# Weight-block sums in the second half of a feed-forward: from GpSimd to VectorE, spread over the steps

## The chip, the cores and the metric

The kernel runs on one core of a Trainium2 chip. The metric is the time of one launch on the device in microseconds (us), given as the median of several runs. Five engines matter here: TensorE (PE, with its weight loads as PEld), VectorE (DVE), ScalarE (ACT), GpSimd (POOL) and the queue SP, which issues all DMAs. Each works through its own instruction list in order and waits on semaphores.

## The reference

The reference is one layer of a hybrid encoder on 1024 tokens of width 1024. What matters here is its feed-forward, with DFF = 2816:

```
hn = rms_norm(h)
ab = hn @ w_in                       # 1024 x 1024 @ 1024 x 5632
a, g = ab[:, :2816], ab[:, 2816:]
u = gelu(causal_dwconv(a)) * g       # 1024 x 2816
h = h + u @ w_out                    # 1024 x 2816 @ 2816 x 1024
```

Attention comes before it; a gate (`sigmoid(rms_norm(h) @ Wg) * (p @ Wp)`) and a last norm come after it. Everything is float32.

## The kernel before

**Precision.** Each float32 operand of a product is split into a high part and a low part. ScalarE copies the operand as the high part (`copy`, L799), VectorE subtracts that from the operand to get the low part (`low`, L1182), and TensorE forms three products of parts (SPLIT3) per block.

**Second half of the feed-forward, `u @ w_out`.** It is done as a fast 2x2 block product with seven products in place of eight. The operands of some of the seven are sums or differences of blocks. For `u` these are formed earlier and stored in memory (`u_ops`). For `w_out` they are formed on the chip out of the 256 KB blocks loaded by `load_b` (L584). The blocks lie in the lists `res[1]` to `res[5]`, 11 blocks in each (NQ = 11); `B_RES` tells which list each of the seven products reads: 1, 3, 4, 1, 5, 2, 3. So `res[1]` is read raw in product 0 and as a sum in product 3, `res[3]` raw in product 1 and as a sum in product 6, `res[5]` and `res[2]` as sums in products 4 and 5.

**Steps.** There are NSTEP = 77 steps, s = 11 r + q, for product r and block q. One step is 12 matmuls of 128x128 by 128x512 on TensorE (`step`, L2048). Before it, TensorE waits for the low parts of the step's two operands (`op_lo`). Operands lie in a ring of nine places. A place is free again when the step that used it is done, so ScalarE and VectorE fill behind TensorE: after TensorE's step s, they fill the weight operand of step s+4 and the `u` operand of step s+5 (`fills_after`). VectorE does, at each step s (L1627 to L1651): some additions of finished products to the residual (`h_adds`, L1602; two a step in steps 11 to 18, one in 22 to 25 and in 33 to 36, two in 44 to 49, one in 55 to 62), then the two fills (`op_lo`, L1421), and in steps 56 to 63 the low part of one block of the gate's weight. `h_adds` of a product come once that product is complete, and product r+2 may not begin before those of product r are done, as it uses the same PSUM banks.

**Loads.** SP goes through one list too (L614 to L647). `load_u(s)` puts the `u` operand of step s into a ring of four places, once VectorE has filled the operand of step s-4. The blocks of `res[4]` and `res[2]` for block q follow `load_u(16 + 3q//2)`. At s = 59 SP waits for all 44 sums (`S.t_low`) and then loads the first block of the gate's weight over the space of `res[1]`, and one more block at each of the next seven steps.

**The sums before.** GpSimd does 44 subtractions of 128x512 as one list (L772 to L785): for each q two of them (`res[5] = res[2] - res[1]`, then `res[1] = res[4] - res[5]`) once the pair of blocks q has landed, then 11 of `res[2] = res[4] - res[2]`, then 11 of `res[3] = res[3] - res[1]`. ScalarE waits for the right count of `S.t_low` before it splits a summed block (L1013). After them GpSimd has only one-column operations for the norms (L678).

Of the kernel before, what the change touches and what calls it, by code (L numbers as in the profile page):

```python
# [31 lines left out]
NF = DFF // P  # L32
# [31 lines left out]
def build(nc, x, p, w_in, w_out, sinks, lambda_q, lambda_k, subln_gain, rel_bias, norm_mix, norm_ffn,  # L64
# [108 lines left out]
    def op(k):  # L173
        return ring_at[k % RING].rearrange("p (l n) -> p l n", l=2)
# [5 lines left out]
    def w_half(f, gate, half):  # L180
        return w_tile(f, gate)[:, HALF_X[half]]
# [6 lines left out]
    def blk_there(eng, q, n):  # L188

        eng.wait_ge(wv_loaded[q], (16 if q < 5 else 0) + 16 * n)  # L190

    def s_tmp(n, f):
        if f == 0 and n <= 2:
            return gel[:, HALF_X[n - 1]]
        return xs[:, (n - 1) // 2, HALF_X[(n - 1) % 2]]
# [15 lines left out]
    NPROD = len(order)  # L211
    nth = {o: i for i, o in enumerate(order)}
    NQ = NF // 2
# [6 lines left out]
    def fills_after(pos):  # L220
        return [k for k in range(RING, NFILL) if user(k - RING) == pos]
# [6 lines left out]
    res = {1: x_blk[0] + x_blk[1][0:3],  # L228
           5: rest[0:NQ],
           4: rest[NQ:] + misc[0:1],  # L230
           3: [wbuf_f[:, 6 * D + HALF * i:6 * D + HALF * (i + 1)] for i in range(8)] + misc[1:4],
           2: [wbuf_f[:, 10 * D + HALF * i:10 * D + HALF * (i + 1)] for i in range(10)] + misc[4:5]}
# [7 lines left out]
    def wg_raw(r):  # L240
        return act_f[:, (KD + r) * SEQ:(KD + r + 1) * SEQ]
# [7 lines left out]
    def u_raw(s):  # L249
        return raw[:, s % 4 // 2, HALF_X[s % 2]]  # L250
# [28 lines left out]
    S = type("S", (), sems)  # L279
# [389 lines left out]
    def _(pool):  # L669
# [6 lines left out]
        def power(src, dst, ready, done, n):  # L676
            pool.wait_ge(ready, n + 1)
            nc.gpsimd.tensor_tensor(dst, src, stat[:, 63:64], ALU.pow).then_inc(done, 1)  # L678
# [25 lines left out]
        def minus(dst, a, b, done):  # L704
            nc.gpsimd.tensor_tensor(dst, a, b, ALU.subtract).then_inc(done, 1)  # L705
# [40 lines left out]
        def su(f):  # L746
            q = f // 2
            pool.wait_ge(S.u_ready, f + 1)
            a0, a1 = u_buf(2 * q), u_buf(2 * q + 1)
            if f % 2 == 0:  # L750
                if q >= 1:
                    pool.wait_ge(S.u_st, 112 * q)
                minus(su_buf(3), a0[:, 0:HALF], a0[:, HALF:SEQ], S.su)
                return
            if q >= 1:
                pool.wait_ge(S.u_st, 112 * q)
            plus(su_buf(1), a0[:, HALF:SEQ], a1[:, HALF:SEQ], S.su)
            if q >= 1:
                pool.wait_ge(S.u_st, 112 * q)
            pool.wait_ge(S.su, 4 * q + 2)  # L760
            minus(su_buf(2), su_buf(1), a0[:, 0:HALF], S.su)
            if q >= 1:
                pool.wait_ge(S.u_st, 112 * q)
            pool.wait_ge(S.su, 4 * q + 3)
            minus(su_buf(4), a1[:, 0:HALF], su_buf(2), S.su)

        for f in range(NF):
# [1 line left out]
                s1(f + 3)  # L769
                s3(f + 3)  # L770
            su(f)
        pool.wait_ge(S.u_st, 112 * NQ)  # L772
        pool.wait_ge(S.c21, NF)
        for q in range(NQ):
            blk_there(pool, q, 4)
            minus(res[5][q], res[2][q], res[1][q], S.t_low)
            pool.wait_ge(S.t_low, 2 * q + 1)
            pool.wait_ge(S.op_lo, NPROD + 2 * q + 2)
            minus(res[1][q], res[4][q], res[5][q], S.t_low)
        for q in range(NQ):  # L780
            minus(res[2][q], res[4][q], res[2][q], S.t_low)
        for q in range(NQ):
            pool.wait_ge(S.t_low, 2 * q + 2)
            pool.wait_ge(S.op_lo, NPROD + 2 * (NQ + q) + 2)
            minus(res[3][q], res[3][q], res[1][q], S.t_low)  # L785

        power(stat[:, 20:21], stat[:, 28:29], S.ms2, S.pow2, 0)
        power(stat[:, 21:22], stat[:, 29:30], S.ms2, S.pow2, 1)
        for t in range(NT + 1):
# [382 lines left out]
    def _(dve):  # L1172
# [7 lines left out]
        def low(dst, src, hi, done, scale=None):  # L1180
            if scale is None:
                ins = nc.vector.tensor_tensor(dst, src, hi.bitcast(F32), ALU.subtract)  # L1182
            else:
                ins = nc.vector.scalar_tensor_tensor(out=dst, in0=src, scalar=scale, in1=hi.bitcast(F32),  # L1184
                                                     op0=ALU.mult, op1=ALU.subtract)
            if done is not None:
                ins.then_inc(done, 1)
            return ins
# [142 lines left out]
        for n in range(NA + 3):  # L1331
            if n < NA:
                s = n // NT
# [72 lines left out]
        def minus(dst, a, b):  # L1406
            return nc.vector.tensor_tensor(dst, a, b, ALU.subtract)  # L1407

        def s2(f):
            dve.wait_ge(S.s1, f + 1)  # L1410
            w_there(dve, f, 0)
            minus(s_tmp(2, f), s_tmp(1, f), w_half(f, 0, 0)).then_inc(S.s2, 1)

        def s4(f):
            if f == 0:
                dve.wait_ge(S.tr1, turn_no[2, 3])
                dve.wait_ge(S.t3_tok, 4)
            dve.wait_ge(S.s2, f + 1)
            minus(s_tmp(4, f), w_half(f, 0, 1), s_tmp(2, f)).then_inc(S.s4, 1)

        def op_lo(k):  # L1421
            if k < NPROD:
                n, f = order[k]
                if n == 6:
                    s2(f)
                    if f >= 1:
                        s4(f)
                if (n, f) == (7, 0):
                    s4(0)
                src = (w_half(f, 0, n - 1) if n in (1, 2) else w_half(f, 1, 1) if n == 4  # L1430
                       else s_tmp({5: 1, 6: 2, 7: 3, 3: 4}[n], f))
            else:
                s = (k - NPROD) // 2
                src = u_raw(s) if k % 2 == NPROD % 2 else res[B_RES[s // NQ]][s % NQ]
            dve.wait_ge(S.op_hi, k + 1)
            low(op(k)[:, 1, :], src, op(k)[:, 0, :], S.op_lo)
# [16 lines left out]
        for i in range(NT):  # L1453
            t, j, b = O_TILE[i], i // 2, 2 * (i % 2)
# [80 lines left out]
        def taps(f):  # L1535
            def tap(n):
                return cols[:, f + NF * n:f + NF * n + 1]
            dve.wait_ge(S.tap0, f + 1)
            link(nc.vector.scalar_tensor_tensor(out=conv[:, :], in0=a_buf[:, 1:1 + SEQ], scalar=tap(1), in1=conv[:, :],
                                                op0=ALU.mult, op1=ALU.add))  # L1540
            nc.vector.scalar_tensor_tensor(out=conv[:, :], in0=a_buf[:, 2:2 + SEQ], scalar=tap(2), in1=conv[:, :],
                                           op0=ALU.mult, op1=ALU.add).then_inc(S.conv_done, 1)

        def gated(f):
            dve.wait_ge(S.gelu_done, f + 1)
            dve.wait_ge(S.c21, f + 1)
            nc.vector.tensor_tensor(u_buf(f), u_buf(f), gel[:, :], ALU.mult).then_inc(S.u_ready, 1)  # L1547
# [54 lines left out]
        def h_adds(r, i0, i1):  # L1602
            for i in range(i0, min(i1, 4 * len(QUADS[r]))):
                m, n = QUADS[r][i // 4]
                t = 4 * m + i % 4
                dve.wait_ge(S.prod, NPROD + NQ * (r + 1))
                if r == 0:
                    dve.wait_ge(x_again[t], 48)
                nc.vector.tensor_tensor(h[:, t, HALF_X[n]], ps[:, banks(r)[i % 4], :], h[:, t, HALF_X[n]], ALU.add  # L1609
                                        ).then_inc(S.h_fin, 1)  # L1610
# [10 lines left out]
        def ple_lo(t):  # L1621
            dve.wait_ge(S.xhi2, t + 1)
            b = 3 if t < 2 else 0
            low(ut[:, t % 2, 1, :], ps[:, b:b + 2, :].rearrange("p b n -> p (b n)"), ut[:, t % 2, 0, :], None)
            low(pt[:, t % 2, 1, :], ps[:, 5 if t < 2 else 2, 0:DPLE], pt[:, t % 2, 0, :], S.xlo2)

        for s in range(NSTEP):  # L1627
            r, q = s // NQ, s % NQ
            if s == 1:
                taps(NF - 1)  # L1630
            if s == 2:
                gated(NF - 1)
            if r == 6:
                if q == 0:
                    h_adds(5, 0, 8)
            elif r >= 1:
                per = (4 * len(QUADS[r - 1]) + 7) // 8
                h_adds(r - 1, per * q, per * (q + 1))
            for k in fills_after(NPROD + s):
                op_lo(k)  # L1640
            if r == 5 and 1 <= q <= KD:
                dve.wait_ge(S.wg_hi, q)
                low(act_t[:, 1, q - 1, :], wg_raw(q - 1), act_t[:, 0, q - 1, :], S.wg_lo)
            if (r, q) == (5, 10):
                ple_norm(0)
            if (r, q) == (6, 4):
                ple_lo(0)
                ple_norm(1)
            if (r, q) == (6, 8):
                ple_lo(1)  # L1650
                ple_norm(2)  # L1651
# [499 lines left out]
```

## Time and profile before

| | |
|---|---|
| median of 3 runs | 1267.37 us (1266.23 to 1270.18) |
| time of the profiled run | 1269.17 us |
| its span, first to last instruction | 1267.3 us |
| mean granted TensorE clock | 0.991 of full speed |
| PE, DVE, ACT, POOL busy | 96%, 69%, 41%, 25% |
| steps 13 to 40 of the second half | 953.39 to 1038.67 us of the span |

The busy shares are averages over the whole span, and so say nothing of a single stretch. The span is the profiled execution's; the time of the same run is 1.9 us longer.

### The profile page before, as it was taken

What the parts mean: (1) busy time and instruction counts of PE and PEld (TensorE: products, weight loads), DVE (VectorE), ACT (ScalarE), POOL (GpSimd) and SP (SyncE); (2) the same over time, 40 slices, a digit from 0 to 9 for tenths busy, and PEclk for the clock granted to TensorE, in tenths of its full rate; (3) what the DMA queues carried; (4) which work ended last, traced back from release to release, by engine and by line L of the source; (5) the groups of instructions that cost most, each with busy time, mean ns of one, the idle gap of its engine ahead of it and who ended that gap; (6) DMA issues with size and microseconds to landing.
All of it is one profiled execution on the core that took longest, in us unless ns stands there. A gap on an engine that the chain in (4) does not pass through costs nothing.

```text
span 1267.3 us, 17105 instructions
## 1 busy us (share of the span) xinstructions
PE 1221.7 (96%) x6167; PEld 1001.0 (79%) x6167; DVE 875.8 (69%) x1466; ACT 518.9 (41%) x1042; POOL 322.9 (25%) x335
## 2 busy tenths in 40 slices
PE   8999999999788999999999999999999999999997
PEld 7997887787667787888888888888887768888885
DVE  5423776776894566877788777787769996864442
ACT  4322664656653233433333333333344344733321
POOL 0000000454553121232331332322217860000000
PEclk9999999999999998999999999999999999999998
DMA  8453233112914312233332333332497434520101
GB/s 223 85 95 72 59 85 75 34 41 73 286 51 101 100 67 65 79 124 101 108 98 86 108 108 100 112 96 84 161 374 237 158 106 143 177 74 25 42 34 50
DMA packets 128669, 136.08 MB, mean 107 GB/s; under 512 B 15570, under 2 KB 93130, under 8 KB 128522
## 3 DMA queue, kind: packets, MB, share of 16 engines
q1 hardware_dynamic: 128586, 135.00, 35.6%
q8 instruction: 49, 0.80, 0.3%
q14 instruction: 34, 0.28, 0.1%
HBM read 96.77 MB, written 37.22 MB: 106 GB/s over the span
## 4 chain that ended last, share of the span: by engine, by line
PE 57%; DVE 8%; issue 3%; DMA 1%; ACT 0%; SPq 0%; POOL 0%; POOLq 0%; DVEq 0%
PE ps L1683 56%; DVE wbuf L1182 4%; DVE more L1182 1%; DVE h L1609 1%; PE ps L1689 1%; DMA act_t<-mix_a 1%; PE ps L1923 0%; DVE xs L1468 0%; DVE h L1463 0%; DVE conv L1407 0%; SPq L479 0%; POOL stat L678 0%; ACT xs L802 0%; DVE act_t L1182 0%; PE ps L2073 0%
## 5 line engine op out<-in xcount | busy, mean ns | idle before, releaser
L1683 PE MATMUL ps<-act_t,wbuf 128*128 128x512 f32 x1200 | 291.2, 399 | 2.9 <-DVE wbuf L1182 2.9
L1683 PEld LDWEIGHTS ps<-act_t,wbuf 128*128 128x128 f32 x1200 | 227.3, 190 | 58.0 <-issue 3.3
L1683 PE MATMUL ps<-wbuf 128*128 128x512 f32 x912 | 217.4, 392 | 3.0 <-DVE wbuf L1182 3.0
L1683 PEld LDWEIGHTS ps<-wbuf 128*128 128x128 f32 x912 | 169.9, 188 | 42.3 <-DVE wbuf L1182 5.7
L1683 PE MATMUL ps<-act_t,wq 128*128 128x512 f32 x624 | 155.7, 402 | 3.6 <-DVE wq L1184 2.8
L1683 PEld LDWEIGHTS ps<-act_t,wq 128*128 128x128 f32 x624 | 114.6, 188 | 33.4 <-issue 7.3
L1182 DVE TENSOR_TENSOR wbuf<-raw,wbuf 128x512 fp32r<-128x512 f32 (+1 forms) x107 | 104.9, 981 | 13.2 <-ACT wbuf L799 12.9
L799 ACT ACTIVATE wbuf<-raw 128x512 fp32r<-128x512 f32 (+1 forms) x107 | 69.2, 649 | 88.4 <-PE ps L1683 65.5
L678 POOL TENSOR_TENSOR stat<-stat 128x1 f32<-128x1 f32 x32 | 17.6, 551 | 343.2 <-DVE stat L1191 343.2
L1683 PE MATMUL ps<-hx,wbuf 128*128 128x512 f32 x408 | 96.2, 391 | 0.0
L1683 PEld LDWEIGHTS ps<-hx,wbuf 128*128 128x128 f32 x408 | 76.5, 188 | 16.6
L1683 PE MATMUL ps<-wbuf,act_t 128*128 128x512 f32 x288 | 73.9, 411 | 3.4 <-DMA act_t<-mix_a 3.4
L881 ACT ACTIVATE e_t<-ps,small 128x128 f32<-128x128 f32 (+7 forms) x64 | 47.4, 741 | 62.5 <-DVE small L1311 61.3
L799 ACT ACTIVATE wbuf<-xs 128x512 fp32r<-128x512 f32 x66 | 39.8, 624 | 76.4 <-DVE xs L1407 54.2
L1683 PEld LDWEIGHTS ps<-wbuf,act_t 128*128 128x128 f32 x288 | 54.8, 195 | 16.6 <-issue 3.8
L1683 PE MATMUL ps<-wq,act_t 128*128 128x384 f32 (+1 forms) x384 | 58.1, 310 | 1.6 <-DVE wq L1182 1.6
L1683 PE MATMUL ps<-act_t,more 128*128 128x512 f32 x240 | 58.2, 395 | 0.0
L1683 PEld LDWEIGHTS ps<-wq,act_t 128*128 128x128 f32 x384 | 56.5, 188 | 2.0 <-issue 1.8
L694 POOL TENSOR_TENSOR o_t<-o_sb 128x128 f32<-128x128 f32 x32 | 14.7, 461 | 167.3 <-ACT o_sb L957 163.1
L705 POOL TENSOR_TENSOR wbuf_f<-wbuf_f 128x512 f32<-128x512 f32 x33 | 52.1, 1579 | 19.0 <-DVE wbuf_f L1547 16.0
L1182 DVE TENSOR_TENSOR a_t<-ps,a_t 128x512 fp32r<-128x512 f32 (+4 forms) x64 | 44.6, 715 | 17.1 <-ACT a_t L799 17.0
L1683 PEld LDWEIGHTS ps<-act_t,more 128*128 128x128 f32 x240 | 45.2, 188 | 10.6
(203 smaller groups left out, 2058.7 us busy)
## 6 DMA issues: line engine op xcount, KB each, us to landing
u_ops<-wbuf_f SPq DMA_DIRECT2D x77, 256.0 KB, 2.2
raw<-u_ops SPq DMA_DIRECT2D x77, 256.0 KB, 2.7
raw<-in_w_ffn_in SPq DMA_DIRECT2D x33, 512.0 KB, 3.9
g_ffn<-in_w_ffn_in SPq DMA_DIRECT2D x11, 512.0 KB, 4.0
act_f<-in_w_ffn_out SPq DMA_DIRECT2D x21, 256.0 KB, 3.8
w_raw<-in_w_in SPq DMA_DIRECT2D x10, 512.0 KB, 4.6
wbuf_f<-in_w_ffn_out SPq DMA_DIRECT2D x18, 256.0 KB, 5.5
x_in<-in_x SPq DMA_DIRECT2D x8, 512.0 KB, 3.6
```

Of the source, the lines that this page charges most:

```text
L678: nc.gpsimd.tensor_tensor(dst, src, stat[:, 63:64], ALU.pow).then_inc(done, 1)
L694: nc.gpsimd.tensor_tensor(o, o_sb[:, 0, :], o_sb[:, 1, :], ALU.add).then_inc(S.b_sum, 1)
L705: nc.gpsimd.tensor_tensor(dst, a, b, ALU.subtract).then_inc(done, 1)
L799: nc.scalar.activation(dst, src, ACT.Copy, scale=scale).then_inc(done, 1)
L881: nc.scalar.activation(e_t[:, pr, m, 0:w], psf[:, at:at + w], ACT.Exp, scale=-1.0, bias=small[:, o + 2 + m:o + 3 + m], accum_out=small[:, ...
L1182: ins = nc.vector.tensor_tensor(dst, src, hi.bitcast(F32), ALU.subtract)
L1609: nc.vector.tensor_tensor(h[:, t, HALF_X[n]], ps[:, banks(r)[i % 4], :], h[:, t, HALF_X[n]], ALU.add).then_inc(S.h_fin, 1)
L1683: return nc.tensor.matmul(dst, lhs, rhs, start=start, stop=stop)
L1689: ins = nc.tensor.transpose(psf[:, bank * HALF + k * P:bank * HALF + (k + 1) * P], src[:, k * P:(k + 1) * P], ident[:, :])
```

## The change

The 44 subtractions leave GpSimd's list, with GpSimd's waits. VectorE does the same 44, each counted on the same semaphore `S.t_low` and each followed by a wait of VectorE for its own count. They are spread over the steps, after the fills of a step: two for block q at step 20 + 3q//2 (steps 20 to 35), one for block q of `res[2]` at step 36 + q//2 (two a step in 36 to 40, one in 41), and one for block q of `res[3]` at step 42 + q (42 to 52). The wait for the pair of blocks (`blk_there(..., q, 4)`) is now VectorE's.

```diff
@@ GpSimd's list
             su(f)
-        pool.wait_ge(S.u_st, 112 * NQ)
-        pool.wait_ge(S.c21, NF)
-        for q in range(NQ):
-            blk_there(pool, q, 4)
-            minus(res[5][q], res[2][q], res[1][q], S.t_low)
-            pool.wait_ge(S.t_low, 2 * q + 1)
-            pool.wait_ge(S.op_lo, NPROD + 2 * q + 2)
-            minus(res[1][q], res[4][q], res[5][q], S.t_low)
-        for q in range(NQ):
-            minus(res[2][q], res[4][q], res[2][q], S.t_low)
-        for q in range(NQ):
-            pool.wait_ge(S.t_low, 2 * q + 2)
-            pool.wait_ge(S.op_lo, NPROD + 2 * (NQ + q) + 2)
-            minus(res[3][q], res[3][q], res[1][q], S.t_low)
-
@@ VectorE's list
+        def w_sum(dst, a, b, n):
+            minus(dst, a, b).then_inc(S.t_low, 1)
+            dve.wait_ge(S.t_low, n)
+
+        def w_sums(s):
+
+            for q in range(NQ):
+                if s == 20 + 3 * q // 2:
+                    blk_there(dve, q, 4)
+                    w_sum(res[5][q], res[2][q], res[1][q], 2 * q + 1)
+                    w_sum(res[1][q], res[4][q], res[5][q], 2 * q + 2)
+            for q in range(NQ):
+                if s == 36 + q // 2:
+                    w_sum(res[2][q], res[4][q], res[2][q], 2 * NQ + q + 1)
+            for q in range(NQ):
+                if s == 42 + q:
+                    w_sum(res[3][q], res[3][q], res[1][q], 3 * NQ + q + 1)
+
         for s in range(NSTEP):
...
             for k in fills_after(NPROD + s):
                 op_lo(k)
+            w_sums(s)
```

## Rows read from the trace of the kernel before

**Rows 1.** The page's part 1: busy time and share of the span.
```profile
PE 1221.7 (96%) x6167; PEld 1001.0 (79%) x6167; DVE 875.8 (69%) x1466; ACT 518.9 (41%) x1042; POOL 322.9 (25%) x335
```
**Rows 2.** Windows: stretch, its length; PE, PEld, DVE, ACT, POOL busy; clock, DMA share, GB/s.
```profile
928.66:953.39 24.73, 24.73 (x109) 20.27 (x108) 15.50 (x20) 10.19 (x18) 4.79 (x3) 1.00 1.02 371
953.39:978.46 25.07, 24.88 (x109) 20.11 (x108) 25.07 (x32) 10.96 (x20) 21.18 (x13) 1.00 0.67 220
978.46:1005.20 26.74, 25.69 (x108) 19.93 (x108) 26.74 (x23) 11.24 (x19) 22.75 (x15) 1.00 0.52 166
1005.20:1035.81 30.61, 27.20 (x108) 19.58 (x108) 30.61 (x23) 11.39 (x19) 30.01 (x18) 1.00 0.34 102
1035.81:1060.64 24.83, 24.83 (x108) 20.39 (x109) 19.79 (x33) 10.15 (x18) 0.00 (x0) 1.00 0.41 122
...
1085.37:1110.10 24.73, 24.73 (x110) 20.27 (x109) 23.36 (x33) 18.08 (x27) 0.43 (x1) 1.00 0.48 141
```
**Rows 3.** The chain that ended last, in order of time: start, length, what.
```profile
1005.15 11.91 DVE wbuf L1182 x7
...
1035.81 82.67 PE ps L1683 x360
```
**Rows 4.** Timeline of DVE: start, length, instruction, [idle before].
```profile
1022.08 1.77 DVE L1182 TENSOR_TENSOR wbuf<-raw,wbuf 128x512 fp32r<-128x512 f32 x1
1023.77 0.68 DVE L1609 TENSOR_TENSOR h<-ps,h 128x512 f32<-128x512 f32 x1
...
1036.28 0.68 DVE L1182 TENSOR_TENSOR wbuf<-act_f,wbuf 128x512 fp32r<-128x512 f32 x1
1036.88 0.68 DVE L1182 TENSOR_TENSOR wbuf<-raw,wbuf 128x512 fp32r<-128x512 f32 x1
```
**Rows 5.** Timeline of POOL: ten of its sums, with no gap between them.
```profile
997.74 17.06 POOL L705 TENSOR_TENSOR wbuf_f<-act_f,wbuf_f 128x512 f32<-128x512 f32 x10
```
**Rows 6.** Line L1407, DVE subtractions of float32: count, duration ns min/median/max, first and last start.
```profile
L1407 DVE TENSOR_TENSOR xs<-raw,xs x21: 691/693/694, 505.2 to 886.8; 128x512 f32<-128x512 f32 x21
...
L1407 DVE TENSOR_TENSOR conv<-xs,conv x4: 1641/1663/1666, 428.1 to 486.9; 128x512 f32<-128x512 f32 x4
```
**Rows 7.** Timeline of DVE, two subtractions of which the second waits for the first.
```profile
504.50 0.68 DVE L1407 TENSOR_TENSOR xs<-xs,raw 128x512 f32<-128x512 f32 x1
505.22 0.69 DVE L1407 TENSOR_TENSOR xs<-raw,xs 128x512 f32<-128x512 f32 x1
```
**Rows 8.** Timeline of POOL beside the first long `conv<-xs,conv`.
```profile
427.37 1.80 POOL L705 TENSOR_TENSOR more_f<-xs 128x512 f32<-128x512 f32 x1 [1.40 <-DVE xs L1468]
```
**Rows 9.** Timeline of DVE at step 66: eight additions, then the next fill.
```profile
1111.46 4.87 DVE L1609 TENSOR_TENSOR h<-ps,h 128x512 f32<-128x512 f32 x8
1116.24 0.68 DVE L1182 TENSOR_TENSOR wbuf<-wbuf_f,wbuf 128x512 fp32r<-128x512 f32 x1
```
**Rows 10.** Timeline of PE over the same stretch.
```profile
1112.85 5.63 PE L1683 MATMUL ps<-wbuf 128*128 128x512 f32 x24
1118.32 0.38 PE L2073 MATMUL ps<-ident,xs 128*128 128x128 f32 x2
```
**Rows 11.** Waits of ACT, 1000 to 1036 us: us in total, times, longest.
```profile
ACT wbuf L799 <- DMA raw<-u_ops: 6.4, 7, 2.0
```
**Rows 12.** Timeline of SP: the pair of blocks q = 8, second load.
```profile
984.28 0.42 SPq L589 DMA_DIRECT2D wbuf_f<-in_w_ffn_out  x1
```
**Rows 13.** Timeline of POOL: the sum that waits for that pair.
```profile
987.83 1.43 POOL L705 TENSOR_TENSOR act_f<-wbuf_f,act_f 128x512 f32<-128x512 f32 x1 [3.28 <-DMA wbuf_f<-in_w_ffn_out]
```
**Rows 14.** Timeline of SP: first load of the gate's weight.
```profile
1068.74 0.38 SPq L647 DMA_DIRECT2D act_f<-in_w_ple_gate  x1
```
**Rows 15.** DMA issues, 1066 to 1095 us: count, KB each, median us to landing.
```profile
act_f<-in_w_ple_gate SPq DMA_DIRECT2D x8, 512.0 KB, 3.6
raw<-u_ops SPq DMA_DIRECT2D x10, 256.0 KB, 2.6
```
**Rows 16.** Timeline of ACT: first split of the gate's weight.
```profile
1083.90 1.05 ACT L799 ACTIVATE act_t<-act_f 128x1024 fp32r<-128x1024 f32 x1
```

## The prediction

> **What bounds the kernel now.** I read the shares of the page first: TensorE is busy for 96% of the span [rows 1], so a gain can only come from what is left of TensorE's idle time, or from matmuls that run faster; the change touches no matmul. The second view is the table of windows, cut so that each holds nine steps of the second half (nine operand places, so the pattern of matmul groups repeats, and a group on the tile `more` opens each window). The steps are numbered back from the transposes at L2073, which stand ahead of step 70. By that the window that opens at 953.39 us holds steps 13 to 21, and the next ones 22 to 30, 31 to 39, and 40 to 48 (from 1035.81). Undisturbed, nine steps take 24.73 us, which is 2.75 us a step [rows 2]. The four windows from 953.39 take 25.07, 26.74, 30.61 and 24.83. Over 24.73 each, that is 0.34 + 2.01 + 5.88 + 0.10 = 8.33 us lost. The granted clock is 1.00 in all of them, so none of it is a clock.
>
> What does TensorE wait for? In the three slow windows VectorE is busy for the whole length, without a gap, and GpSimd for 21 to 30 us; in the windows after them GpSimd does nothing and VectorE has gaps again [rows 2]. The chain of waits says the same: from 1005.15 it runs through VectorE's fills, and from 1035.81 through 82.67 us of matmuls alone [rows 3]. So here VectorE sets the step. Why it does, its timeline shows. A fill whose two inputs lie in SBUF takes 0.68 us from 1036 on, and the next starts 0.60 us after it; while GpSimd works, the same instruction takes 1.77 us and the next starts 1.70 us on [rows 4]. GpSimd's ten sums take 17.06 us, which is 1.70 each, without a gap [rows 5]. The two run in turns, at the same 1.70 us. An addition with one input in PSUM keeps its 0.68 us in the same stretch [rows 4]. So the cost is a turn taken with GpSimd over SBUF operands, and two fills at 1.70 us make a step of 3.40 us where TensorE needs 2.75.
>
> **What is removed.** All 44 sums leave GpSimd, and in this stretch it has nothing else. Every fill from step 13 on then costs 0.60 us. VectorE is no longer the last to arrive by this cause, and all 8.33 us come back if what is added fits.
>
> **What is added.** 44 subtractions of 128x512 float32 on VectorE, each with a wait for its own end. The operation is in the trace: 0.69 us with both inputs in SBUF [rows 6], and from one to the next that waits for it 0.72 us (504.50 to 505.22) [rows 7]. The lower bound of the price is the 0.60 us of instructions that don't wait [rows 4], the upper one the 1.66 us of the four `conv<-xs,conv` [rows 6]. Beside the first of those a GpSimd subtraction runs from 427.37 for 1.80 us [rows 8]; that is the same turn-taking, and after the change GpSimd has none in this stretch. I take 0.72: 44 x 0.72 = 31.7 us of VectorE, over steps 20 to 52.
>
> The page VectorE: DVE Perf Modes of the Trainium skill, section "The DRAIN you can't avoid", says that a semaphore after every operation costs nothing extra. By that the 44 would take 44 x 0.60 = 26.4 us. The row with the wait shows 0.12 us more for each; the row decides, and either fits.
>
> Does it fit? TensorE gives VectorE 24.73 us for nine steps. Each nine have 18 fills, 10.8 us. Steps 13 to 21: 12 additions at 0.60 (7.2) and 4 sums (2.9), 20.9 us. Steps 22 to 30: 4 additions (2.4), 12 sums (8.6), 21.8. Steps 31 to 39: 4 additions (2.4), 14 sums (10.1), 23.3. Steps 40 to 48: 10 additions (6.0), 10 sums (7.2), 24.0. The last four sums (steps 49 to 52) meet few additions. So each window fits, the fullest with 0.7 us over. In the trace VectorE was 23.36 us busy in a window of nine steps in which TensorE lost nothing [rows 2], so a share like this is no trouble by itself.
>
> Inside a window it is uneven. The worst run is steps 44 to 49: 12 fills (7.2), 12 additions (7.2), 6 sums (4.3) = 18.7 us against 6 x 2.75 = 16.5, so VectorE falls 2.2 us behind. A fill after step s is wanted at the start of step s+4, three steps or 8.2 us later. That there is room is seen at step 66: VectorE does eight additions in one go, 4.87 us, the next fill starts only at 1116.24 [rows 9], and the matmuls run on from 1112.85 for 5.63 us up to the transposes at 1118.32 [rows 10], the window before them being a clean 24.73 [rows 2]. A lag of 2.2 us is under that 4.87. I count no loss.
>
> Queued behind VectorE's new waits are its own fills and, by these, TensorE. Its own count comes at once. The wait for the pair of blocks: the loads for q follow `load_u(16 + 3q//2)`, which goes out when VectorE has filled the operand of step 12 + 3q//2, that is after its step 7 + 3q//2; the sums stand at step 20 + 3q//2, 13 steps or 36 us later. The pair q = 8 was issued at 984.28 [rows 12] and had landed when GpSimd took it at 987.83 [rows 13]: 3.5 us. So this wait is over long before. Nothing of ScalarE's waits on the sums: they stand at least four steps ahead of its split.
>
> One queue is moved past: SP waits for all 44 sums ahead of the gate's weight. Before, that was done when SP came by at 1068.74 [rows 14], at VectorE's step 50. Now it ends with VectorE's step 52, some 6.2 us later, and the loads of `u` for steps 60 and on stand behind it. On the old time scale the first gate block lands at 1074.9 + 3.6 = 1078.5 [rows 15], and ScalarE wants it at 1083.90 [rows 16]. The `u` of step 60 lands 2.6 us after that [rows 15], at 1081.1, about when ScalarE turns to it (after step 55, some 3 us ahead of that split), and TensorE needs it four steps, 11 us, later. I cost it at nothing; without that cover it would be some 0.5 us.
>
> **The sum.** On the profiled run's own time: 1269.17 - 8.33 = 1260.8 us; its span would go from 1267.3 to 1259.0. The profiled run is 1.8 us above the median of the runs shown, so the median becomes 1267.37 - 8.33 = 1259.0. Own range 1257.3 to 1261.0, for the spread of the runs shown (1266.23 to 1270.18).
>
> **Rivals.**
>
> *Loads hold the early windows.* The losses of 0.34 and 2.01 us stand beside a DMA share of 0.67 and 0.52, and ScalarE waited 6.4 us in seven goes for `u` operands from 1000 to 1036 [rows 2, 11]. If loads and not VectorE made the two early losses, they stay, and 5.98 us come back: 1261.4. Against it: the window from 928.66 has a DMA share of 1.02 and loses nothing [rows 2]; and a `u` load goes out only after a fill of VectorE, so ScalarE's wait follows VectorE's lag.
>
> *The sums are dear on VectorE, and it gets slower.* The mechanism is VectorE's in-order list in steps 22 to 48: 54 fills, 18 additions and 36 sums of x us. That is 43.2 + 36x against 27 x 2.75 = 74.2 us plus the 4.9 us of lag shown to be harmless, 79.1. Loss begins at x = 1.0, and beyond x = 1.23 it eats the 8.33 us. At 1.70 us, the price beside GpSimd, it is 43.2 + 61.2 - 79.1 = 25.3 us lost, net 17.0 slower: 1284.3. For it speaks that four rows do stand at 1.66 us; against it that the first of them has a GpSimd partner [rows 8], and 21 rows of one operation lie between 0.691 and 0.694 [rows 6].
>
> *The change doesn't give back what it should.* VectorE's stretched fills might be an effect of where the operands lie, not of GpSimd, and steps stay at 3.40 us. Then nothing is won, and the sums come on top, in part within lag: no change at best, 1267.4. Against it: the same `wbuf<-raw,wbuf` is at 1.77 and 0.68 us within 15 us of each other [rows 4].
>
> **Chances.** Forecast 0.80; loads in the early windows 0.10; no change 0.05; dear sums 0.05. The measurement can tell about 0.3%, 3.8 us, so faster means below 1263.6: 0.91, within 0.3%: 0.05, slower 0.04 (of the dear sums, a fifth would stop short of slower). The range holds the forecast and the rival at 1261.4 with the spread of the runs: 1256.5 to 1262.5.
>
> **What would show it.** Right: the windows of nine steps from step 13 all at 24.7 to 24.9 us; fills at 0.68 us with no 1.7 among them from there on; 44 new instructions of 0.69 us on VectorE, at the line of its subtraction helper; GpSimd idle from the last `su` to the norms; VectorE with small gaps of waiting for ScalarE in steps 13 to 52, fewest in 40 to 49; the chain of waits on matmuls from before 953 to the end. Wrong: matmul gaps released by fills in steps 40 to 50 (lag too long), or about step 60 (SP's wait), or sums over 1 us, or fills still at 1.7 us with GpSimd silent.

## The result, and the profile after

| | before | after |
|---|---|---|
| median, the 7 runs taken together | 1271.86 us (1266.23 to 1272.56) | 1261.3 us (1256.78 to 1263.67) |
| ratio, 95% interval | | 0.9935 (0.9916 to 0.9954) |
| profiled run, its span | 1269.17, 1267.3 us | 1262.01, 1259.9 us |
| step 13 to the transposes ahead of step 70 | 164.93 us | 156.59 us |

The kernel is faster by 0.65% and the interval excludes no change. (The ratio is an estimate over all the runs; the two medians alone give 0.9917, just inside the interval.) A repeat with 7 runs of it against 20 of the kernel before gave 0.9941 (0.9917 to 0.9966). The last row of the table is the sharpest measure, and the experiments are read by it: from the matmul that opens step 13 (953.39 before, 954.27 after) to the transposes at L2073 or L2077 (1118.32 and 1110.86). It fell by 8.34 us.

The windows of nine steps, cut as in [rows 2], in the kernel after (columns: stretch, length; PE, PEld, DVE, ACT, POOL busy; clock, DMA share, GB/s):

```profile
954.27:979.00 24.73, 24.73 (x109) 20.27 (x108) 22.16 (x37) 10.69 (x19) 0.00 (x0) 1.00 0.83 282
979.00:1003.73 24.73, 24.73 (x110) 20.27 (x108) 21.81 (x35) 10.38 (x18) 0.00 (x0) 1.00 0.56 171
1003.73:1028.45 24.72, 24.72 (x109) 20.27 (x108) 22.58 (x37) 10.40 (x18) 0.00 (x0) 1.00 0.35 101
1028.45:1053.18 24.73, 24.73 (x109) 20.27 (x108) 22.83 (x37) 10.39 (x18) 0.00 (x0) 1.00 0.32 96
```

Before the change they took 25.07, 26.74, 30.61 and 24.83 us. TensorE is now busy for the whole of each, GpSimd does nothing, and VectorE is busy for 22 to 23 of 24.7 us.

The chain that ended last, against [rows 3], is matmuls from before the sums up to the transposes:

```profile
849.86 261.17 PE ps L1687 x1137
```

VectorE's timeline (start, length, instruction) has two fills and the two sums of one q; it answers to [rows 4, 7]. Fills are at 0.69 us, and a sum that the next instruction waits for takes 0.72 us from start to start, as taken:

```profile
1005.27 0.69 DVE L1167 TENSOR_TENSOR wbuf<-raw,wbuf 128x512 fp32r<-128x512 f32 x1
1005.87 0.69 DVE L1392 TENSOR_TENSOR act_f<-wbuf_f,act_f 128x512 f32<-128x512 f32 x1
1006.59 0.69 DVE L1392 TENSOR_TENSOR act_f<-act_f 128x512 f32<-128x512 f32 x1
```

SP's wait for all 44 sums, against [rows 14], shows in its timeline: the gate's first load goes out 112.76 us after the start of step 13. Before, it went out 115.35 us after it, or 107.0 with the 8.34 us taken off. So it is 5.7 us later on the same scale (6.2 were forecast), and TensorE lost nothing by it.

```profile
1067.03 0.33 SPq L647 DMA_DIRECT2D act_f<-in_w_ple_gate  x1
1067.45 0.38 SPq L582 DMA_DIRECT2D raw<-u_ops  x1
```

### The profile page after: what moved, and what is told of

It reads as the page before. It is cut to its first block, busy times and chain, and to the rows that moved or that the text cites. A ratio compares the mean times of both kernels' runs of the same rounds, so it can differ in the third digit from the quotient of the medians.

```text
span 1259.9 us, 17110 instructions
## 1 busy us (share of the span) xinstructions
PE 1219.5 (97%) x6167; PEld 1004.0 (80%) x6167; DVE 868.3 (69%) x1510; ACT 517.3 (41%) x1042; POOL 248.5 (20%) x291
## 4 chain that ended last, share of the span: by engine, by line
PE 63%; issue 2%; DVE 2%; DMA 1%; SPq 0%; ACT 0%; POOL 0%; POOLq 0%; DVEq 0%
PE ps L1687 62%; PE ps L1693 1%; DMA act_t<-mix_a 1%; DVE xs L1453 0%; PE ps L1927 0%; DVE h L1448 0%; DVE conv L1392 0%; SPq L479 0%; POOL stat L678 0%; ACT xs L787 0%; DVE act_t L1167 0%; PE ps L2077 0%; DVE gel L1680 0%; DVE h L1669 0%; DVE conv L1666 0%
## 5 line engine op out<-in xcount | busy, mean ns | idle before, releaser
L1167 DVE TENSOR_TENSOR wbuf<-raw,wbuf 128x512 fp32r<-128x512 f32 (+1 forms) x107 | 87.6, 819 | 13.4 <-ACT wbuf L784 13.1
L1666 DVE TENSOR_TENSOR conv<-ps,conv 128x1024 f32<-128x1024 f32 x8 | 9.8, 1225 | 62.1 <-PE ps L1687 62.1
```

The source lines that it names most:

```text
L1666: nc.vector.tensor_tensor(conv[:, :], ps[:, 5:7, :].rearrange("p b n -> p (b n)"), conv[:, :], ALU.mult).then_inc(S.gated, 1)
```

## The experiments

All are edits of the kernel after. "The stretch" is the one of the table's last row. It does not move with the level of a run: it was 156.59 us in the kernel after and again in its repeat. So I read a difference of 0.1 us in it, while the ratios of whole runs have intervals 0.26 to 0.55% wide. Each kernel has one profiled execution; that the stretch repeats rests on the kernels that agree in it to 0.02 us.

| kernel | stretch, us | over the kernel after | ratio to before (95%) |
|---|---|---|---|
| before | 164.93 | 8.34 | 1 |
| again (repeat) | 156.59 | 0.00 | 0.9941 (0.9917 to 0.9966) |
| nosum | 156.59 | 0.00 | 0.9944 (0.9924 to 0.9965) |
| half_pool | 158.63 | 2.04 | 0.996 (0.9941 to 0.998) |
| t3_vector | 156.59 | 0.00 | 0.9936 (0.9912 to 0.996) |
| pool_memset | 156.58 | -0.01 | 0.9939 (0.9925 to 0.9954) |
| pool_one_in | 173.76 | 17.17 | 1.008 (1.0063 to 1.0097) |
| pool_sub | 185.60 | 29.01 | 1.0177 (1.015 to 1.0205) |
| dear128 | 159.93 | 3.34 | one run, 1263.72 against 1265.87 us |
| dear256 | 165.59 | 9.00 | 1.0016 (1.0003 to 1.0029) |
| dear512 | 177.06 | 20.47 | 1.0122 (1.0094 to 1.0149) |
| burst11 | 156.61 | 0.02 | one run, 1258.20 against 1265.87 us |
| burst22 | 166.54 | 9.95 | 1.0041 (1.0024 to 1.0058) |

**The repeat.** No edit.

> The changed kernel, unchanged, to tighten its ratio to the kernel before. Theory (turns with GpSimd gone, sums fit): 8.3 us less than before, ratio 0.9935, and every window of nine steps from step 13 on at 24.7 us. Rival (part of the 7-run difference is the level of the runs, not the change): a ratio nearer to 0.998 or to 0.990, outside 0.992 to 0.995.

It came out as the theory has it, in the stretch to 0.01 us.

**Do the sums on VectorE cost anything?**

```diff
-    B_RES = (1, 3, 4, 1, 5, 2, 3)
+    B_RES = (1, 3, 4, 1, 2, 2, 3)
...
-                    sp.wait_ge(S.t_low, 4 * NQ)
...
-                    elif r == 2:
+                    else:
                         blk_there(act, q, 4)
-                    else:
-                        act.wait_ge(S.t_low, {3: 2 * q + 2, 4: 2 * q + 1, 5: 2 * NQ + q + 1, 6: 3 * NQ + q + 1}[r])
...
-            if r == 0:
-                act.wait_ge(S.t_low, 4 * NQ)
...
-            w_sums(s)
```

> Leaves out the 44 sums altogether (products 3 to 6 read blocks as loaded; product 4 reads the blocks of res[2], since nothing writes res[5]), and the waits on them. Theory: the sums on VectorE cost nothing, so it takes as long as the changed kernel, within 0.1% (1.3 us), ratio to before 0.9935. Rival (the sums still cost something, by lag or by SP's wait for all 44): faster than the changed kernel by over 2 us, ratio below 0.992.

The stretch takes 156.59 us, the same as with the sums. They and SP's wait are wholly covered, and nothing is left to win in this stretch by making them cheaper. The median of its whole runs is even 3.0 us above the repeat's (1261.86 against 1258.87), which is the level of the runs and not the sums.

**Part of the change alone.** GpSimd keeps its first loop (two sums for each q), VectorE has the other 22.

```diff
+        for q in range(NQ):
+            blk_there(pool, q, 4)
+            minus(res[5][q], res[2][q], res[1][q], S.t_low)
...
+            minus(res[1][q], res[4][q], res[5][q], S.t_low)
...
-                    w_sum(res[5][q], res[2][q], res[1][q], 2 * q + 1)
-                    w_sum(res[1][q], res[4][q], res[5][q], 2 * q + 2)
+                if s == 36 and q == 0:
+                    dve.wait_ge(S.t_low, 2 * NQ)
```

> One part of the change alone: the first 22 sums (the two of each q) stay on GpSimd as before, the later 22 are on VectorE. Theory (VectorE pays a turn for each GpSimd sum, and TensorE loses what is over VectorE's room): the windows of steps 13 to 30 lose 0.3 to 0.5 and 1.5 to 2.1 us as before, those from step 31 on nothing, so 1.8 to 2.6 us over the changed kernel, ratio to before about 0.9955, and fills at 1.77 us only up to about 998 us. Rival (the early losses came from loads): the same times, but the changed kernel would show those losses too, and it does not; rival (the turns cost in proportion): half of 8.3, 4.2 us over the changed kernel.

The stretch is 2.04 us over the kernel after, within the 1.8 to 2.6 expected, and far from the 4.2 of a proportional cost. (The whole runs can't tell the two apart: the ratios are 0.996 and 0.9941, the medians 4.4 us from each other.) Its windows of nine steps, columns as above:

```profile
951.18:977.71 26.53, 24.91 (x110) 20.07 (x108) 26.53 (x33) 11.95 (x21) 22.18 (x14) 1.00 0.66 222
977.71:1002.68 24.97, 24.97 (x109) 20.27 (x110) 24.29 (x27) 10.09 (x17) 13.88 (x9) 1.00 0.62 189
1002.68:1027.40 24.72, 24.72 (x109) 20.27 (x108) 17.14 (x27) 10.38 (x18) 0.00 (x0) 1.00 0.40 128
```

The split over the two windows was expected as in [rows 2] (0.3 to 0.5, then 1.5 to 2.1) and came out as 1.80 and 0.24. That part was a miss; the sum over both windows was not. Most of the difference is one fill at the border of the windows, for which TensorE waits. In half_pool it met a sum of GpSimd, before it did not:

```profile
975.81 1.75 DVE L1175 TENSOR_TENSOR more<-act_f,more 128x512 fp32r<-128x512 f32 x1
```
```profile
977.64 0.68 DVE L1182 TENSOR_TENSOR more<-act_f,more 128x512 fp32r<-128x512 f32 x1
```

What matters is that TensorE loses only what is beyond VectorE's room: half the sums cost a quarter of the loss (2.04 of 8.34), and the rest falls on the second half, when the room is used up.

**What takes the turn?** Three kernels give GpSimd work back from step 13 or 14 on, with VectorE still doing the sums. Each has one of these lines, in a loop of 44, 100 or 120, in this order:

```diff
+            link(nc.gpsimd.tensor_tensor(xs[:, 0, 0:HALF], g_ple[:, 0:HALF], g_ple[:, HALF:D], ALU.subtract))
+            link(nc.gpsimd.tensor_scalar(xs[:, 0, 0:HALF], g_ple[:, 0:HALF], 1.0, EPS, ALU.mult, ALU.add))
+            link(nc.gpsimd.memset(xs[:, 0, 0:HALF], 0.0))
```

> The changed kernel plus 44 GpSimd subtractions of 128x512 with two SBUF inputs, a constant tile into a scratch place, from step 13 on: turns are back and the sums are on VectorE too. Theory of turns: a VectorE fill or sum beside them takes 1.7 us in place of 0.69, 44 of them, for about 75 us; 22 to 34 us over the changed kernel. Rival (the 1.7 us came from the sums' own operands, such as the same blocks read by both engines, and not from GpSimd at work on SBUF): fills stay at 0.69 us, and the time is that of the changed kernel.

> The changed kernel plus 100 GpSimd tensor_scalar operations of 128x512 from step 13 on: one SBUF input. If reading is what takes the turn: fills are stretched by the duration of one such operation (0.7 to 1.2 us), so to 1.3 to 1.9 us, and 20 us or more over the changed kernel. If only two GpSimd inputs do it: fills at 0.69 us and the changed kernel's time.

> The changed kernel plus 120 GpSimd memsets of 128x512 into the scratch place from step 13 on: GpSimd writes SBUF and reads nothing. If a turn is taken for reading only: fills stay at 0.69 us, time that of the changed kernel. If any GpSimd work on SBUF takes the turn: each fill waits out a memset (some 0.6 us), fills near 1.2 us, and 5 to 20 us over the changed kernel.

The same fill, `wbuf<-raw,wbuf`, in VectorE's timeline (start, length, instruction) of pool_sub, pool_one_in and pool_memset, in this order:

```profile
1005.41 1.77 DVE L1173 TENSOR_TENSOR wbuf<-raw,wbuf 128x512 fp32r<-128x512 f32 x1
```
```profile
1003.47 1.09 DVE L1173 TENSOR_TENSOR wbuf<-raw,wbuf 128x512 fp32r<-128x512 f32 x1
```
```profile
1000.31 0.68 DVE L1173 TENSOR_TENSOR wbuf<-raw,wbuf 128x512 fp32r<-128x512 f32 x1
```

In each, ScalarE also waits for the added work before the norm that uses `xs` next. The work was over by 1054.06 us at the latest, and all of TensorE's waits up to the transposes are for fills of VectorE, so this wait is not in the numbers.

GpSimd's added group in pool_one_in and in pool_memset (behind the first bar its busy us and the mean ns of one, behind the second the idle time before it):

```profile
L775 POOL TENSOR_SCALAR xs<-g_ffn 128x512 f32<-128x512 f32 x100 | 90.4, 904 | 30.8 <-DVE h L1600 22.7
```
```profile
L775 POOL MEMSET xs<- 128x512 f32 x120 | 63.2, 527 | 29.2 <-DVE h L1600 22.3
```

Two GpSimd inputs: the fill is back at 1.77 us, though GpSimd's operands have nothing to do with the sums, and 29.01 us are lost. So it is GpSimd's work, not where the sums' blocks lie. One input: 1.09 us and 17.17 us lost, less than the 20 or more and the 1.3 to 1.9 us expected. No input, 120 writes back to back: 0.68 us and nothing lost. So VectorE's fill is stretched beside GpSimd operations that read SBUF, and not beside writes. It is stretched more by those with two inputs than by those with one, but these are also longer: GpSimd's 44 took 74.93 us, 1.70 each, its 100 took 98.61 us, 0.99 each, and VectorE's fills beside them started 1.70 and 1.02 us apart. Which of the two sets the stretch, number or length, is not separated.

The page SBUF — State Buffer of the Trainium skill, section "SBUF: two separate sides", says that GpSimd and a VectorE operation with two SBUF inputs exclude each other, the latter only against a GpSimd operation that reads SBUF. The three rows of the fill agree, the memset's 0.68 us above all.

The 29.01 us lost in pool_sub lie in the expected 22 to 34 in part by luck. TensorE's waits for fills are 16.9 us of them. The other 12.2 are longer matmuls (TensorE is busy for 168.75 us of the stretch in place of 156.59), above all at a lower granted clock (0.94 over the stretch), which the expectation left out. PE's timeline and a window over its first group, in pool_sub:

```profile
995.43 4.61 PE L1693 MATMUL ps<-wbuf 128*128 128x512 f32 x12 [3.68 <-DVE wbuf L1173]
1002.18 4.60 PE L1693 MATMUL ps<-more,wbuf 128*128 128x512 f32 x12 [2.14 <-DVE more L1173]
```
```profile
995.40:1000.10 4.70, 4.61 (x12) 3.31 (x12) 4.67 (x3) 0.03 (x1) 4.46 (x4) 0.64 0.22 56
```

**The price at which the change turns bad.** A further VectorE subtraction, waited for, behind each sum (128, 256 or 512 columns; `w` below):

```diff
             dve.wait_ge(S.t_low, n)
+            link(minus(xs[:, 0, 0:w], g_ple[:, 0:w], g_ple[:, HALF:HALF + w]))
```

> Doubles the price of a sum: behind each of the 44 a further VectorE subtraction of 128x512 into a scratch place, waited for, so x = 1.44 us. The prediction's rule for steps 22 to 48 (43.2 + 36x against 74.2 plus the room) gives 95.0 against 79.1 with the 4.9 us of room shown: 15.9 us over the changed kernel; with a room of 6.4 us (8.2 less the 1.8 that a fill takes after its step) 14.4 us; net slower than before by 6 to 8 us. Rival (VectorE has more room than the sum says): under 8 us over the changed kernel, so no slower than before.

> The same with a subtraction of 128x256, about 0.33 us and the wait: x near 1.17 us. Rule: 43.2 + 42.1 = 85.3 against 79.1: 6.2 us over the changed kernel with a room of 4.9 us, 4.7 with 6.4. Rival (more room): nothing lost.

> Behind each of the 44 sums a VectorE subtraction of 128x128, about 0.33 us with its wait, so x near 1.05 us. Counted over steps 20 to 52, the load is 51.6 + 44x against 33 x 2.75 = 90.7; the two dearer runs then leave a room of 5.4 and 4.9 us. Theory (that rule with a room of 5.1): 97.8 - 90.7 - 5.1 = 2.0 us over the changed kernel's 156.59 us of the stretch, 1.0 to 3.0. Rival (the room is the 8.2 us of one go): nothing lost.

A sum and its addition in dear512, VectorE's timeline:

```profile
1001.34 0.69 DVE L1392 TENSOR_TENSOR act_f<-wbuf_f,act_f 128x512 f32<-128x512 f32 x1
1002.07 0.69 DVE L1392 TENSOR_TENSOR xs<-g_ffn 128x512 f32<-128x512 f32 x1
1002.79 0.69 DVE L1392 TENSOR_TENSOR act_f<-act_f 128x512 f32<-128x512 f32 x1
```

From start to start the two take 1.45 us together, and 1.19 and 1.04 us in dear256 and dear128. Lost are 20.47, 9.00 and 3.34 us, more than the first rule gave (15.9 and 6.2) and more than the mended one (2.0, at most 3.0). The mended rule had a slip: by the measured 1.45 and 1.19 us the two dearer runs leave a room of 4.2 and 4.3 us, not 5.4 and 4.9, and it then gives 2.9. Between dear128 and dear256 each 0.15 us a sum cost 5.66 us, and 44 sums x 0.15 is 6.6: most of what is added reaches TensorE. As an estimate, drawn back at 44 us per us from 3.34, the loss starts at 1.04 - 3.34/44 = 0.96 us a sum, and between the two runs the 8.34 us are used up at 1.17 or so. The sums cost 0.72, so the margin would be some 0.24 us each; no run lies inside it.

**The room.** The 22 sums of the later lists, or 11 of them, in one go at step 38:

```diff
-                if s == 36 + q // 2:
+                if s == 38:
...
-                if s == 42 + q:
+                if s == 38:
```

> The 22 later sums in one go at step 38, 15.8 us of VectorE, in place of steps 36 to 52: it measures the room. Theory with the room of three steps and a fill's slack in the next (the weight fill of step 43 is then done some 18.2 us after step 38, and TensorE wants it 11.0 us after): 7.2 us over the changed kernel, in one gap ahead of step 43. If only the 4.9 us shown at step 66 are harmless: 10.9 us. Rival (room is no limit, since the average fits): nothing.

> Only the 11 sums of res[2] in one go at step 38 (8.0 us), in place of steps 36 to 41; the last 11 stay at steps 42 to 52. In the burst of 22 the weight fill of step 43 came 7.67 us late after 15.9 us of sums, so 8.2 us of a burst were covered. Theory (room in one go 8.2 us): the stretch from the start of step 13 to the transposes ahead of step 70 takes the changed kernel's 156.59 us, within 0.2. Rival (only the 4.9 us shown at step 66 are harmless): 3.1 us more, 159.7.

Burst22, PE's timeline (in brackets the idle time before):

```profile
1028.99 5.62 PE L1687 MATMUL ps<-wbuf 128*128 128x512 f32 x24
1042.29 5.02 PE L1687 MATMUL ps<-wbuf 128*128 128x512 f32 x12 [7.67 <-DVE wbuf L1167]
```

The one gap is ahead of step 43 and 7.67 us long, near the 7.2 expected; and 8.0 us in one go (burst11) cost 0.02 us. So the room in one go is 22 x 0.72 - 7.67 = 8.2 us, and the 4.9 us taken from step 66 were only its lower bound. The loss of burst22 is still 9.95 us, not 7.2, because the twelve matmuls behind the gap take 5.02 in place of 2.92 us, at a granted clock of 0.57:

```profile
1042.20:1047.40 5.20, 5.11 (x14) 4.05 (x15) 4.25 (x8) 0.05 (x1) 0.00 (x0) 0.57 0.55 134
```

That is between the levels of 1.2 and 2.4 GHz; TensorE had been idle for the 7.67 us before, and the clock was not in the expectation.

**The same change elsewhere.** The four GpSimd subtractions beside the norms (427 to 490 us) go to VectorE:

```diff
-                if i >= 3:
-                    pool.wait_ge(S.tr1, turn_no[3, i // 2 - 1])
-                minus(t_tmp[3], xs[:, 1, HALF:D], xs[:, 1, 0:HALF], S.t3_tok)
...
+                minus(t_tmp[3], xs[:, 1, HALF:D], xs[:, 1, 0:HALF]).then_inc(S.t3_tok, 1)
```

> The same change at another place: the four GpSimd subtractions into more_f beside the norms (427 to 486 us), which stretch VectorE's conv<-xs,conv to 1.66 us, go to VectorE too, behind its own three. Theory of turns: conv<-xs,conv falls from 1.66 to 0.69 us each, VectorE reaches the next fill 0.4 us earlier each time, so 0.4 to 1.6 us less than the changed kernel. Rival (not on TensorE's path there): same as the changed kernel, and conv<-xs,conv at 0.69 us all the same. If conv<-xs,conv stays at 1.66 us, the theory of turns is wrong.

VectorE's timeline of t3_vector, against the 1.66 us of [rows 6]:

```profile
430.16 0.69 DVE L1389 TENSOR_TENSOR conv<-xs,conv 128x512 f32<-128x512 f32 x1
430.89 0.69 DVE L1389 TENSOR_TENSOR a_buf<-xs,conv 128x512 f32<-128x512 f32 x1
431.50 0.69 DVE L1389 TENSOR_TENSOR more_f<-xs 128x512 f32<-128x512 f32 x1
```

From the first addition to `h` to the first `a_buf<-ps` it takes 73.52 us (420.40 to 493.92), where before, after and again took 74.17, 74.15 and 74.18. So 0.65 us are won, at the low end of 0.4 to 1.6. It is on TensorE's path: the group of matmuls that waits for a fill at the end of this part starts 71.10 us after that addition, against 71.74 before, and its wait is 2.54 in place of 2.90 us (PE's timeline, t3_vector and before):

```profile
491.50 4.58 PE L1685 MATMUL ps<-act_t,wbuf 128*128 128x512 f32 x12 [2.54 <-DVE wbuf L1164]
```
```profile
490.02 5.46 PE L1683 MATMUL ps<-act_t,wbuf 128*128 128x512 f32 x12 [2.90 <-DVE wbuf L1182]
```

The length of this group itself is the clock's, and differs from run to run (last section). In the ratio of whole runs 0.65 us can't be told (0.9936 against 0.9941). As far as the traces show it is the best version here; the times of whole runs can't confirm it.

## Why the prediction was right or wrong

- *VectorE sets the step while GpSimd works, by turns over SBUF operands.* Right. Shown by the windows after, by pool_sub (turns back, 16.9 us of waits for fills) and pool_memset (no reading, no turn).
- *8.33 us come back.* Right: 8.34 in the stretch. nosum shows that this is all there is.
- *The early losses of 0.34 and 2.01 us too* (the rival at 1261.4 us kept them as the loads' doing). They went, with a DMA share of 0.83 and 0.56 in these windows. The rival fell, though 1261.3 us is what the median says; it agrees by chance.
- *A sum costs 0.72 us, and the load fits.* Right (0.72; over the four windows VectorE is busy for 89.4 us where the prediction added up 90.0). The worst run and its room were right in kind: the 8.2 us that the prediction names as three steps is what burst11 and burst22 measure, and the 4.9 us it leaned on was a lower bound.
- *SP's wait costs nothing.* Right (5.7 us later, nothing lost).
- *From the stretch to the time.* This is the step that failed: the term 1267.37 in "the median becomes 1267.37 - 8.33", and the own range of 1257.3 to 1261.0 drawn from the same three runs. It took the median and the spread of three runs as the level of the kernel. With four more runs that median was 1271.86, and the kernel after had 1261.3: 2.3 above the forecast of 1259.0, inside the wide range of 1256.5 to 1262.5 and outside the own one. The medians of the two differ by 10.56 us, where the traces give 8.34 and the ratio of 0.9935 stands for 8.2 to 8.3 (forecast: 1259.0/1267.37 = 0.9934). In later series the kernel before had 1268.73, 1267.43 and 1267.2, and the repeat 1258.87, so one series of seven is itself off by some us.
- *What moved the level.* "1269.17 - 8.33 = 1260.8" failed in the same way: the profiled run after took 1262.01. Of the 1.2 us, 0.88 lie ahead of step 13, which starts at 953.39 before and 954.27 after, with the same code ahead, and 0.24 in the part of the time outside the span. From the transposes to the end of the span it is 149.0 us in both. So the step that failed is not in the stretch that the change touches. Part of the spread ahead of it is the clock (last section); why four of the seven runs of before lay near 1272 stays open, since none of them has a trace.
- *The price of dear sums.* The rule of the slower rival was mis-sized. It counted steps 22 to 48 and a room of 4.9 us; the sums of steps 20, 21 and 49 to 52 belong to the same queue. For 1.44 us it gave 15.9 where 20.47 were measured; counted over steps 20 to 52 it gives 19.4. Its point of turning, 1.23 us, is nearer to 1.17. Why a steady load leaves a room of about 4 us, when a single burst has 8.2, stays open.

## What to carry to other kernels

Before giving elementwise work to GpSimd because it is idle, look at the length of VectorE's instructions while it runs: where those with two SBUF inputs are stretched and those with a PSUM input are not, the work is paid for twice, and 44 sums of 0.72 us on VectorE are cheaper than 44 turns, each of which costs VectorE 1.10 us (1.70 less 0.60) where it meets a fill. Spread such work over the steps, and count VectorE's load for as many steps as the consumer's pattern repeats; a burst is free up to the room that the ring gives (8.2 us here). And measure a small change in its own stretch: 8.34 us showed there to 0.01 us, while whole runs of one kernel lay up to 11.6 us apart (the kernel before, 1263.38 to 1274.95 in one series of 20).

## What the runs showed of the hardware

**The clock behind a wait differs from run to run.** At about 490 us TensorE waits 2.90 us for the same fill in each kernel, with the same code ahead. Granted clock and length of the stretch with the twelve matmuls behind it, in the kernels before, after and again:

```profile
490.00:495.30 5.30, 5.28 (x13) 4.03 (x14) 2.38 (x4) 0.63 (x1) 0.00 (x0) 0.50 0.00 0
```
```profile
492.40:496.60 4.20, 4.18 (x13) 3.29 (x14) 2.37 (x4) 0.63 (x1) 0.00 (x0) 0.66 0.00 0
```
```profile
489.90:492.80 2.90, 2.87 (x12) 2.32 (x13) 2.14 (x4) 0.63 (x1) 0.00 (x0) 1.00 0.00 0
```

A clock of 0.50 (the level of 1.2 GHz) for all of it, of 0.66, and of 1.00 (2.4 GHz). This alone is 2.4 us between two runs. Step 13 starts at 953.39 before, 954.27 after, 950.50 in again and 957.01 in nosum, and from the transposes to the end of the span it is 149.0 us in all four. So the spread of these four executions, other than the 8.34 us, lies ahead of the stretch; in the stretch itself the clock is 1.00 in all of them. It is not all clock: ahead of 480 us TensorE's one wait for `mix_a` is 3.4 us in again and 5.2 in nosum, and its waits for `xs` are 0.8 and 4.6 us.

**VectorE's wait for GpSimd has steps, and shows as duration.** 1.77 us beside two-input operations, 1.09 beside one-input ones, 0.68 beside memsets, for one and the same fill. The wait stands in the length of the VectorE instruction and not as idle time before it, so VectorE looked busy for 30.61 of 30.61 us [rows 2], though its fills there took 1.77 us for what takes 0.68 us alone.
